# A two-layer diffusion trunk on one NeuronCore: the latent columns of layer 1 computed second, their steps run between the key and value units, and four modulation units placed in attention

## The chip, the cores and the metric

One core of one Trainium2 chip runs the whole program in one launch. The metric is device time in microseconds (us), the median of the runs, and every time below is from the kernel before unless it says otherwise. The engines are PE (TensorE: matmuls and transposes), DVE (VectorE), ACT (ScalarE), POOL (GpSimd) and SP (SyncE, which here only issues DMAs). Each engine works through its own instructions strictly in program order and meets the others at semaphores.

## The reference, cut to what matters

Two layers over 256 image tokens and 256 context tokens of 1024 features. Layer 0 is an even mixer and a dense feed-forward part, layer 1 an odd mixer and eight experts. The change lies in the odd mixer and in the modulation vectors of layer 1:

```python
# odd mixer: h, hc are the modulated tokens of image and context
p, pc = h @ w_in, hc @ w_in            # 1952 columns: q_c k_c v_c (512 each), cq 256, ckv 128, kr 32
q_d = rmsnorm(cq, gq) @ w_uq           # 4 heads of 64 + 32; the 32 are rotated
kv  = rmsnorm(ckv, gkv) @ w_ukv        # 4 heads: 64 of key, 128 of value
k_d = concat(key part, kr)             # kr is shared by the heads, rotated for image tokens
o_c = neighbourhood_attention(q_c, k_c, v_c, ..., rpb)   # 8 heads, with a position bias
o_d = attention(q_d, k_d, v_d)                           # 4 heads, without bias
y   = concat(o_c, o_d) @ w_out
# modulation: six vectors of 1024 per layer, for image and context
mod = silu(c) @ w_mod[l] + b_mod[l]
x   = x + g1 * rmsnorm(y);  h = rmsnorm(x) * (1 + sc2) + sh2;  x = x + g2 * rmsnorm(moe(h))
```

## The kernel before

**Weights as units.** Nearly all weights pass through SBUF in units of 1 MB (128 partitions x 2048 floats). `weight_units` (L100) lists them in order. SP loads them in that order into six raw slots: the load of unit r waits until unit r - 6 is released (L249 to L259). A unit of kind "split" is released when DVE has split it, a "mod" unit when PE has multiplied it, the "latent" unit when the last of its twelve products is done (semaphore `mla_full` at 12, L255). SP issues in order, so a load that waits holds back all that follow it, the bias loads among them.

**Split units.** A weight unit of 256 columns is split into a high and a low part so that three fast matmuls (L478 to L480) make one precise product. ACT writes the high half-unit (`act_split`, L451), DVE the low one (`dve_split`, L460). There are two split slots, so the splits of the unit after next wait for PE to finish this one (`half_free`, L442). PE runs a unit in `gemm_unit` (L493), ACT evicts its two PSUM banks and counts `od_evac`.

**The odd projection.** Eight units `od` 0 to 7: queries 0 and 1 (image tokens only, computed together while the modulated tokens arrive), keys 2 and 3, values 4 and 5, `cq` in 6 (image tokens only, so half the columns), `ckv` and `kr` in 7. A full unit streams 512 token columns, units 0, 1 and 6 stream 256. In the unit list the four modulation units 36 to 39 stand behind unit 1, 40 to 43 behind unit 7, then the latent unit (`w_uq` and `w_ukv`), then the output projection `odo`, then modulation units 44 to 47.

**Between projection and attention** each engine does, in order: ACT squares `cq` and `ckv` (L1039), PE sums them with a matmul by ones (L345), ACT takes the root (L340), DVE the reciprocal (L369) and scales. PE multiplies modulation units 40 to 43 (`pe_mod_rows`, L533; ACT copies the rows, L565; `pe_mod_turn`, L545, turns them), DVE adds the bias and forms the affine vectors. PE makes the twelve latent products (L1582 queries, L1586 keys, L1588 values), each waiting for ACT's eviction two back. Then eight rotations: PE matmul (L775), three DVE steps (L785 to L788): four queries, and the same rotated key once for each of four heads. Then attention starts.

**Attention** has 24 units in layer 1: 16 with the neighbourhood bias, 8 without. In iteration i PE runs the scores of unit i + 1 (L623), the transposes of unit i - 1 (L638) and, in odd iterations, the value product of a pair (L648). DVE scales and adds the bias (L698, L700), takes the maximum (L703, or L707 without bias), ACT the exponential (L663), DVE normalises (L726). The bias of each unit is fetched by two 64 KB DMAs on SP (`load_bias`, L851), which from the third unit on wait until the unit two back has used its buffer, and masked by POOL in two steps (L900, L902). `load_bias` stands ahead of modulation unit 44, that is behind all four `odo` units.

## Time and profile before

| | |
|---|---|
| median of 3 runs | 2098.78 us (2098.07 to 2099.05) |
| profiled execution, first to last instruction | 2095.1 us, 3.7 us below the median; its time outside that span is not shown |
| busy over the span | PE 1955.3 us (93%), DVE 1323.1 (63%), ACT 1112.9 (53%), POOL 28.5 (1%) |
| mean granted clock of PE | 0.964 |
| HBM read | 471.25 MB, 225 GB/s over the span |

The stages: layer 0 up to about 745 us, modulation and first norm of layer 1 to 755, odd projection to 831.5, small steps to 865.6, attention to 950.5, output projection, norms and router to about 1014, experts to the end. A share of busy time is a mean over stages with different limits; what a change in one stage is worth is read from what waits last there. "PEclk" is the clock that the throttle granted to PE: 1.00 is 2.4 GHz, 0.50 is 1.2 GHz. Matmuls are shown with their latency, so consecutive ones overlap a little, and a precise (float32) matmul shows as two records.

### The profile page before, as it was taken

To read this page: it belongs to the slowest core of one execution; us is meant where nothing else is said; L and a number is where in the kernel's file an instruction comes from. 1 tells how busy PE (TensorE), PEld (TensorE's weight loads), DVE (VectorE), ACT (ScalarE), POOL (GpSimd) and SP (SyncE) were. 2 spreads that over 40 slices of the span, in tenths; PEclk is the share of its full clock that TensorE was granted. 3 is DMA by queue.
4 is the path that set the end of the run, shared out by engine and by line. 5 is a ranking of instruction groups with operands and counts; after the bars stand their busy time and mean duration, and the time that the engine had idled before them with its cause. 6 is when DMAs were issued, how large, how long until landed. Compare 5 with 4: busy or idle time off the path is not lost.

```text
span 2095.1 us, 25387 instructions
## 1 busy us (share of the span) xinstructions
PE 1955.3 (93%) x9566; PEld 1537.2 (73%) x9566; DVE 1323.1 (63%) x1263; ACT 1112.9 (53%) x1126; POOL 28.5 (1%) x44
## 2 busy tenths in 40 slices
PE   5998798999999989888799999999999999999996
PEld 3876475888878768347788787887878878788785
DVE  2344735322323361464688888888888888888885
ACT  3533535222223252354477677767767777776773
POOL 0000000000000000120000000000000000000000
PEclk9998889999999999799699999999999999999998
DMA  9453153632222272221499898998989989899991
GB/s 316 139 161 121 32 189 101 201 99 84 100 86 96 72 233 72 78 63 62 159 355 364 317 355 314 360 361 319 362 306 371 363 304 368 307 360 344 331 368 43
DMA packets 263893, 473.27 MB, mean 226 GB/s; under 512 B 17112, under 2 KB 116368, under 8 KB 263824
## 3 DMA queue, kind: packets, MB, share of 16 engines
q1 hardware_dynamic: 262928, 469.31, 63.8%
q0 software_dynamic: 896, 3.02, 0.5%
q8 instruction: 46, 0.75, 0.2%
q14 instruction: 23, 0.19, 0.0%
HBM read 471.25 MB, written 1.05 MB: 225 GB/s over the span
## 4 chain that ended last, share of the span: by engine, by line
PE 82%; DVE 9%; ACT 4%; issue 4%; DMA 1%; DVEq 0%; SPq 0%; ACTq 0%
PE bank L478 23%; PE bank L480 23%; PE bank L479 23%; PE bank L345 2%; PE bank L541 2%; PE bank L648 2%; PE bank L1664 2%; DVE split_low L1414 2%; DMA raw_weights<-in_w_mod 1%; PE bank L1706 1%; PE bank L623 1%; DVE y L1401 1%; PE bank L638 1%; DVE overlay L419 1%; DVE small L707 1%
## 5 line engine op out<-in xcount | busy, mean ns | idle before, releaser
L1414 DVE TENSOR_TENSOR split_low<-raw_weights,split_high 128x2048 fp32r<-128x2048 f32 x224 | 511.6, 2287 | 59.5 <-ACT split_high L1113 58.6
L1113 ACT ACTIVATE split_high<-raw_weights 128x2048 fp32r<-128x2048 f32 x224 | 429.0, 1918 | 147.4 <-PE bank L480 147.3
L462 DVE TENSOR_TENSOR split_low<-raw_weights,split_high 128x1024 fp32r<-128x1024 f32 x118 | 143.9, 1225 | 330.4 <-ACT split_high L457 330.3
L478 PE MATMUL bank<-h_high,split_high 128*128 128x512 f32 (+1 forms) x848 | 326.2, 385 | 23.4 <-DVE h_low L392 10.6
L479 PE MATMUL bank<-h_low,split_high 128*128 128x512 f32 (+1 forms) x848 | 321.4, 379 | 0.0
L480 PE MATMUL bank<-h_high,split_low 128*128 128x512 f32 (+1 forms) x848 | 321.3, 379 | 0.0
L1414 DVE TENSOR_TENSOR h_low<-raw_weights,h_high 128x2048 fp32r<-128x2048 f32 x112 | 256.6, 2291 | 78.1 <-ACT h_high L1113 78.1
L478 PE MATMUL bank<-split_high,xe_high 128*128 128x512 f32 x672 | 271.7, 404 | 14.3 <-DVE split_low L1414 14.3
L480 PE MATMUL bank<-split_high,xe_low 128*128 128x512 f32 x672 | 266.2, 396 | 0.0
L479 PE MATMUL bank<-split_low,xe_high 128*128 128x512 f32 x672 | 266.1, 396 | 0.0
L1113 ACT ACTIVATE h_high<-raw_weights 128x2048 fp32r<-128x2048 f32 x112 | 214.7, 1917 | 43.0 <-PE bank L480 43.0
L457 ACT ACTIVATE split_high<-raw_weights 128x1024 fp32r<-128x1024 f32 x118 | 123.7, 1054 | 203.5 <-PE bank L480 199.5
L478 PEld LDWEIGHTS bank<-h_high,split_high 128*128 128x128 f32 x848 | 162.0, 191 | 57.7 <-issue 22.1
L479 PEld LDWEIGHTS bank<-h_low,split_high 128*128 128x128 f32 x848 | 162.1, 191 | 30.1 <-issue 1.2
L480 PEld LDWEIGHTS bank<-h_high,split_low 128*128 128x128 f32 x848 | 161.7, 191 | 29.4
L478 PEld LDWEIGHTS bank<-split_high,xe_high 128*128 128x128 f32 x672 | 127.0, 189 | 48.0 <-DVE split_low L1414 20.5
L480 PEld LDWEIGHTS bank<-split_high,xe_low 128*128 128x128 f32 x672 | 126.8, 189 | 30.3
L479 PEld LDWEIGHTS bank<-split_low,xe_high 128*128 128x128 f32 x672 | 127.1, 189 | 27.9
L478 PE MATMUL bank<-h_high,xe_high 128*128 128x512 f32 x224 | 89.2, 398 | 3.9 <-DVE h_low L1414 3.9
L478 PE MATMUL bank<-split_high,gt_high 128*128 128x512 f32 x224 | 89.2, 398 | 0.0
L480 PE MATMUL bank<-h_high,xe_low 128*128 128x512 f32 x224 | 88.6, 395 | 0.0
L480 PE MATMUL bank<-h_high,gt_low 128*128 128x512 f32 x224 | 88.5, 395 | 0.0
(236 smaller groups left out, 2711.7 us busy)
## 6 DMA issues: line engine op xcount, KB each, us to landing
raw_weights<-in_moe_w SPq DMA_DIRECT2D x336, 1024.0 KB, 7.1
raw_weights<-in_w_mod SPq DMA_DIRECT2D x48, 1024.0 KB, 6.8
raw_weights<-in_ffn_w SPq DMA_DIRECT2D x33, 1024.0 KB, 5.3
raw_weights<-in_ev_w_in SPq DMA_DIRECT2D x10, 1024.0 KB, 11.9
raw_weights<-in_od_w_in SPq DMA_DIRECT2D x8, 1024.0 KB, 9.7
raw_weights<-in_ev_w_out SPq DMA_DIRECT2D x4, 1024.0 KB, 11.2
raw_weights<-in_od_w_out SPq DMA_DIRECT2D x4, 1024.0 KB, 6.8
overlay<-in_rpb SPq DMA_DIRECT2D x32, 64.0 KB, 2.3
```

The costliest lines, as they stand in the source:

```text
L345: pe.matmul(n["sums"], ones, n["sq"][:, t % 2, :n["width"]], start=(t == 0), stop=(t == n["nt"] - 1)).then_inc(S("squares_used"), 1)
L419: dve.tensor_tensor(TMP[:, t % 2, :wd], n["src"](t), RS[:, :wd], ALU.mult)\
L457: act.activation(half_of(s, j, SPH[:, s % NSPLIT, :]), half_of(s, j, raw_of(r)), ACT.Copy)\
L462: dve.tensor_tensor(half_of(s, j, SPL[:, s % NSPLIT, :]), half_of(s, j, raw_of(split_at[s])), half_of(s, j, SPH[:, s % NSPLIT, :]).bitcast ...
L478: pe.matmul(ps, wh, xh, start=first, stop=False)
L479: pe.matmul(ps, wh, xl, start=False, stop=False)
L480: return pe.matmul(ps, wl, xh, start=False, stop=last)
L541: last = pe.matmul(PS[bank][32 * j:32 * j + 32, 256 * (i % 2):256 * (i % 2) + 256], SC[:, 4 * h + j, :], wt[:, 4 * h + j, :], start=(h == ...
L648: last = pe.matmul(pair_out(units, p)[0], u["v"][kt], PT[p % 2][:, kt, :], start=(kt == 0), stop=(kt == u["nk"] - 1))
L1113: act.activation(esplit(u)[0], RAW[:, u % NRAW, :], ACT.Copy).then_inc(S("e_high"), 1)
L1414: dve.tensor_tensor(lo, RAW[:, u % NRAW, :], hi.bitcast(F32), ALU.subtract)\
L1664: last = pe.matmul(PS[XBANK[r]][:, P * f:P * f + P], half[:, t, k:k + P], rhs, start=(n == 0), stop=(n == 3))
```

## The change

The units of the odd projection are computed in the order 0, 1, 6, 7, 2, 3, 4, 5. Everything that hangs on units 6 and 7 moves into the loop over the units, at positions p (0 to 7) of that order:

- ACT squares `cq` right after unit 6 (p = 2) and `ckv` after unit 7 (p = 3). PE sums `cq` ahead of the unit at p = 4 and `ckv` ahead of p = 5; root, reciprocal and scaling follow at the same positions.
- The rotary key is rotated once, on its own 32 rows (PE at p = 5, ahead of the unit; DVE behind it), and ACT copies the result to heads 1 to 3 at p = 6. Before, it was copied to four heads first and rotated four times.
- The latent products 0 to 7 run ahead of the unit at p = 6, products 8 to 11 and the four query rotations ahead of p = 7. Products now use PSUM banks 2 and 3.
- Attention on PE now waits for four rotations, the spread key, product 12's eviction and the last unit's eviction (`od_evac` 16).
- Modulation units 40 to 43 are multiplied inside attention, in iterations 4, 6, 10 and 12, ahead of the value product's place and behind the transposes; the first turn in iteration 10, the second in 16. ACT copies the rows in iterations 9 and 15, DVE adds bias and affine in iteration 21. The output projection waits for them.
- In the load order the latent unit stands behind the unit at p = 4, modulation units 40 to 43 behind the last unit; `load_bias` stands ahead of the third `odo` unit instead of ahead of modulation unit 44.

```diff
+OD_ORDER = (0, 1, 6, 7, 2, 3, 4, 5)
-    for s in range(8):
+    for s in OD_ORDER:
         units.append(("split", "od", cols(od, min(256 * s, OD_IN - 256))))
         if s == 1:
             units += mods(36, 40)
+        if s == 2:
+            units.append(("latent", "latent", [(0, (2, 384), w["mla_w_uq"][0].rearrange("(k p) n -> p k n", p=P)),
+                                               (768, (768,), w["mla_w_ukv"][0])]))
     units += mods(40, 44)
-    units.append(("latent", "latent", [(0, (2, 384), w["mla_w_uq"][0].rearrange("(k p) n -> p k n", p=P)),
-                                       (768, (768,), w["mla_w_ukv"][0])]))
...
# SP
-                if r == mod_at[44]:
+                if r == split_at[of["odo"][2]]:
                     load_bias()
...
+        KROT = KD[64:96, 0, CTX:TOK]
+        def pe_key_rope(pe):
+            pe.wait_ge(S("od_evac"), 8)
+            pe.matmul(PS[4][64:96, :SEQ], CON[64:96, C_R1 + 64:C_R1 + 96], KROT, start=True, stop=True)\
+              .then_inc(S("key_rot"), 1)
+        def dve_key_rope(dve):
+            t1, t2 = Y[64:96, 6, 0:256], Y[64:96, 6, 256:512]
+            dve.wait_ge(S("key_rot"), 1)
+            dve.tensor_tensor(t1, PS[4][64:96, :SEQ], TAB[64:96, 3, :], ALU.mult)
+            link(dve, dve.tensor_tensor(t2, KROT, TAB[64:96, 2, :], ALU.mult))
+            dve.tensor_tensor(KROT, t1, t2, ALU.add).then_inc(S("key_roped"), 1)
+        def act_key_spread(act):
+            act.wait_ge(S("key_roped"), 1)
+            for h in range(1, 4):
+                last = act.activation(KD[64:96, h, :], KD[64:96, 0, :], ACT.Copy)
+            last.then_inc(S("key_spread"), 1)
...
# ACT, loop over the units (act_latent evicts products i0 to i1 as before)
+            for g, p, s in run_od():
                 to(min(g + 1, of["od"][-1]))
+                if p == 4:
+                    act_root(act, N["cq"])
+                if p == 5:
+                    act_root(act, N["ckv"])
+                if p == 6:
+                    act_key_spread(act)
+                    act_latent(0, 8)
+                if p == 7:
+                    act_latent(8, 12)
...
+                if s == 6:
+                    act_squares(act, N["cq"])
+                if s == 7:
+                    act_squares(act, N["ckv"])
...
+                if i in (9, 15):
+                    act_mods(act, 20 + i // 15, 21 + i // 15, 3)
...
# DVE
+            for g, p, s in run_od():
+                to(min(g + 1, of["od"][-1]))
+                if p == 2:
+                    dve_mods(dve, 8, 10, 7)
+                    dve_affine(dve, 1, 1, 0.0, 16)
+                if p == 4:
+                    dve_latent("cq", V_GQ, 2)
+                if p == 5:
+                    dve_key_rope(dve)
+                    dve_latent("ckv", V_GKV, 1)
+                if p == 7:
+                    dve_rope(dve, 1, range(4))
...
+                if i == 21:
+                    dve_mods(dve, 10, 11, 1)
+                    dve_affine(dve, 1, 2, 1.0, 32)
...
# PE, loop over the units
+                if p == 4:
+                    pe.wait_ge(S("mod_evac"), 10)
+                    pe_sums(pe, N["cq"])
+                if p == 5:
+                    pe_sums(pe, N["ckv"])
+                    pe_key_rope(pe)
+                if p == 6:
+                    pe_latent(0, 8)
+                if p == 7:
+                    pe_latent(8, 12)
+                    pe.wait_ge(S("key_roped"), 1)
+                    pe_rope(pe, 1, lambda i: (S("mla_evac"), i + 1), range(4))
...
+            pe.wait_ge(S("roped1"), 4)
+            pe.wait_ge(S("key_spread"), 1)
+            pe.wait_ge(S("mla_evac"), 12)
+            pe.wait_ge(S("od_evac"), 16)
+            def mods_between(i):
+                if i in (4, 6, 10, 12):
+                    if i == 10:
+                        pe_mod_turn(pe, 20, 1)
+                    pe_mod_rows(pe, 40 + (4, 6, 10, 12).index(i), 3)
+                if i == 16:
+                    pe_mod_turn(pe, 21, 1)
```

## Rows read from the trace of the kernel before

**Rows 1.** The page, part 4: the chain that ended last, by engine.
```profile
PE 82%; DVE 9%; ACT 4%; issue 4%; DMA 1%; DVEq 0%; SPq 0%; ACTq 0%
```

**Rows 2.** Windows by stage: stretch, length, busy (instructions) of five engines, PEclk, DMA, GB/s.
```profile
769.62:831.52 61.90, 61.90 (x384) 55.76 (x384) 13.52 (x12) 16.09 (x23) 0.00 (x0) 1.00 0.30 98
831.52:865.65 34.13, 25.54 (x135) 12.02 (x134) 15.86 (x32) 11.91 (x23) 2.86 (x4) 0.91 0.32 101
865.65:950.51 84.86, 71.90 (x240) 35.51 (x240) 49.68 (x123) 37.71 (x84) 20.56 (x28) 0.84 0.18 47
1040.00:2095.00 1055.00, 1023.79 (x4678) 829.78 (x4676) 882.92 (x548) 738.19 (x507) 0.00 (x0) 0.99 0.90 328
```

**Rows 3.** Timeline, projection to attention: start, length, engine, line, [idle before <- releaser].
```profile
831.56 2.04 ACT L1036 ACTIVATE overlay<-bank 32x512 f32<-32x512 f32 x4 [4.87 <-PE bank L480]
834.19 2.50 PE L345 MATMUL bank<-y,constants 128*128 128x256 f32 x6 [2.66 <-ACT y L332]
...
838.49 3.34 DVE L369 RECIPROCAL y<-y 128x512 f32<-128x512 f32 x1
840.46 1.93 PE L541 MATMUL bank<-raw_weights,silu_c 128*32 128x256 f32 x32 [0.82 <-ACT mod_row_buffers L565]
842.32 1.95 PE L549 MATMUL bank<-constants,mod_row_buffers 128*128 128x2 f32 x16
844.13 3.67 PE L1582 MATMUL bank<-overlay,raw_weights 128*96 128x256 f32 x16
...
851.35 3.80 PE L1588 MATMUL bank<-raw_weights,overlay 128*128 128x512 f32 x8
855.83 1.10 PE L775 MATMUL bank<-overlay,constants 96*96 96x256 f32 x4 [0.69 <-ACT overlay L1053]
858.23 0.64 PE L775 MATMUL bank<-overlay,constants 96*96 96x256 f32 x2 [0.48 <-DVE y L785]
```

**Rows 4.** The unit loop: one wait (total, times, longest), and the opening splits.
```profile
PE bank L478 <- DVE split_low L462: 1.6, 1, 1.6
768.34 4.88 DVE L462 TENSOR_TENSOR split_low<-raw_weights,split_high 128x1024 fp32r<-128x1024 f32 x4 [2.08 <-ACT split_high L457]
```

**Rows 5.** Timeline: SP's issues, and POOL's first masking step.
```profile
838.61 3.34 SPq L816 DMA_DIRECT2D raw_weights<-in_od_w_out  x3
841.99 38.34 SPq L861 DMA_DIRECT2D overlay<-in_rpb  x12
851.89 0.72 POOL L900 TENSOR_TENSOR overlay<-overlay,constants 128x256 f32<-128x256 f32 x1 [808.62 <-DMA overlay<-in_rpb]
```

**Rows 6.** Attention's opening, and PE's gap before transposes at half and full clock.
```profile
865.65 3.78 PE L623 MATMUL bank<-overlay 64*128 64x512 f32 x4 [1.86 <-DVE overlay L788]
869.32 1.28 ACT L663 ACT_TABLE_LOAD   x1 [13.54 <-DVE small L703]
890.63 1.12 PE L638 MATMUL bank<-constants,y 128*128 128x128 f32 x4 [0.35 <-DVE y L726]
905.27 0.66 PE L638 MATMUL bank<-constants,y 128*128 128x128 f32 x4 [1.49 <-DVE y L726]
```

**Rows 7.** The chain in attention: start, length, what; transposes two units before those of rows 6.
```profile
880.51 1.12 PE bank L638 x4
...
898.50 0.66 PE bank L638 x4
```

**Rows 8.** Windows of the granted clock, attention of layer 0 and of layer 1.
```profile
194.00:210.00 16.00, 12.57 (x37) 5.83 (x37) 11.50 (x31) 8.02 (x24) 0.00 (x0) 0.50 0.00 1
864.00:893.00 29.00, 24.14 (x45) 9.62 (x46) 14.45 (x37) 9.31 (x19) 8.15 (x11) 0.50 0.14 28
894.00:950.00 56.00, 46.25 (x192) 25.16 (x191) 35.80 (x90) 27.90 (x65) 11.62 (x16) 1.00 0.21 57
```

**Rows 9.** Two gaps of PE (timeline) that half clock followed.
```profile
194.89 0.80 PE L623 MATMUL bank<-overlay 64*128 64x256 f32 x2 [2.32 <-DVE modulation L571]
954.79 0.42 PE L478 MATMUL bank<-h_high,split_high 128*128 128x256 f32 x1 [4.29 <-DVE split_low L462]
```

More of the change, by code:

```diff
@@ L615, in pair_out, with pe_attention @@
             return PS[OBANK[p % 2]][u["o"], :2 * P], (u["o"], t, slice(c, c + 2 * P))
-        def pe_attention(pe, a, units):
+        def pe_attention(pe, a, units, between=lambda i: None):
             def scores(i):
@@ L640, in pe_attention @@
                     last.then_inc(S(f"ptrans{a}"), 1)
+                between(i)
                 if i >= 3 and i % 2 == 1:
@@ L650, in pe_attention, with act_attention @@
                     last.then_inc(S(f"o{a}"), 1)
-        def act_attention(act, a, units):
+        def act_attention(act, a, units, between=lambda i: None):
             for i in range(len(units) + 3):
+                between(i)
                 if i < len(units):
@@ L680, in act_attention, with dve_attention @@
                     act.activation(HH[dst], src, ACT.Copy).then_inc(S("o_high"), 1)
-        def dve_attention(dve, a, units):
+        def dve_attention(dve, a, units, between=lambda i: None):
             lag = 3 + a
             for i in range(len(units) + lag):
+                between(i)
                 if i < len(units):
@@ L766, in ropes @@
             r, c, s = CON[0:96, C_R1:C_R1 + 96], TAB[0:96, 2, :], TAB[0:96, 3, :]
-            return [(QD[0:96, h, :], r, c, s) for h in range(4)] + [(KD[0:96, h, CTX:TOK], r, c, s) for h in range(4)]
+            return [(QD[0:96, h, :], r, c, s) for h in range(4)]
         def pe_rope(pe, l, ready, tiles=range(8)):
@@ L1015, in _, with act_latent @@
             act_modulate(act, N["n4"], 1, 0, 0)
-            for g, s in run("od"):
-                to(min(g + 1, of["od"][-1]))
+            def act_latent(i0, i1):
+                for i in range(i0, i1):
+                    act.wait_ge(S("mla_full"), i + 1)
+                    b = PS[2 + i % 2]
+                    if i < 4:
+                        act.activation(QD[0:96, i, :], b[0:96, :SEQ], ACT.Copy).then_inc(S("mla_evac"), 1)
+                    elif i < 8:
+                        act.activation(KD[0:64, i - 4, :], b[0:64, :], ACT.Copy).then_inc(S("mla_evac"), 1)
+                    else:
+                        act.activation(VD[:, i - 8, :], b[:, :], ACT.Copy).then_inc(S("mla_evac"), 1)
+            for g, p, s in run_od():
+                to(min(g + 1, of["od"][-1]))
+                if p == 4:
[7 more added lines that the diff above has]
+                    act_latent(8, 12)
                 for j in range(2):
@@ L1553, in _, with pe_latent @@
             pe_mods(pe, 36, 40, 5, 7)
-            for g, s in run("od"):
-                if s == 0:
+            r = latent_at
+            uq, ukv = raw_of(r)[:, 0:768].rearrange("p (k n) -> p k n", k=2), raw_of(r)[:, 768:1536]
+            def pe_latent(i0, i1):
+                for i in range(i0, i1):
+                    if i == 0:
+                        pe.wait_ge(S(f"raw{r % NRAW}"), need[r])
+                        pe.wait_ge(S("latent"), 1)
+                    if i == 4:
+                        pe.wait_ge(S("latent"), 2)
+                    if i >= 2:
+                        pe.wait_ge(S("mla_evac"), i - 1)
+                    else:
+                        pe.wait_ge(S("od_evac"), 4)
+                    b = PS[2 + i % 2]
+                    if i < 4:
+                        for k in range(2):
+                            last = pe.matmul(b[0:96, :SEQ], uq[:, k, 96 * i:96 * i + 96], CQ[:, k, :],
+                                             start=(k == 0), stop=(k == 1))
+                    elif i < 8:
+                        c = 192 * (i - 4)
+                        last = pe.matmul(b[0:64, :], ukv[:, c:c + 64], CKV, start=True, stop=True)
+                    else:
+                        last = pe.matmul(b[:, :], CKV[:, P * (i - 8):P * (i - 7)],
+                                         ukv.rearrange("p (h n) -> p h n", h=4)[:, :, 64:192], start=True, stop=True)
+                    last.then_inc(S("mla_full"), 1)
```

85 lines of the change are left out of this document (18 added, 67 removed).

## The prediction

> **What bounds the kernel now.** I read the page's chain first [rows 1]: TensorE (PE) carries 82% of the time that decides the end, and every share is an average over stages. So I cut the span around the change into stages [rows 2]. The reader is to see four things. While the units of layer 1's input projection run (769.62 to 831.52 us), PE is busy for 61.90 of 61.90 us, so work put in there is paid unless it replaces a wait. Between the last of these matmuls and the first score of attention lie 34.13 us with PE busy for 25.54: small dependent steps, all on the end's path. Attention takes 84.86 us, with PE busy 71.90 but at a mean granted clock of 0.84. The experts after it move 328 GB/s and hold PE at 97%; they follow attention in the program, so what is won before them should shift them as a block. Then I read the 34 us instruction by instruction [rows 3], the waits of the unit loop [rows 4], the DMA queue [rows 5], attention's opening and gaps [rows 6, 7] and the clock [rows 8, 9].
>
> **What the change takes away.** All of the 34.13 us between the last projection matmul and the first score: norm sums, four modulation units, twelve latent products, eight rotations. The loop of units itself keeps its matmuls; only their order changes. The one unit with 256 token columns (half as long as the others) now comes first after the opening pair. The loop is five full units and that half one, so 61.90 / 5.5 = 11.3 us for a full unit and 5.6 for the half. The splits of its successor must be ready after those 5.6 us. Now the four splits behind the opening pair run on VectorE from 768.34 to 773.2 and would be needed from about 775 on; only 1.6 us of waiting shows in the whole loop [rows 4]. I cost the reordering at 0, with up to 2 us if that cover fails.
>
> **What comes back inside the loop, on PE** (durations at full clock from [rows 3]):
> - Norm sums: the row says 2.50 us with a part at half clock and a short wait inside; I take 2.0. The squares are made two units earlier, under a matmul unit.
> - Key rotation: one matmul like those of the rotations, of which two take 1.10, so 0.55. Its three VectorE steps and the copies to the other heads lie beside the next unit.
> - Latent products 0 to 7: 7.2 us, from the first's start at 844.13 to the start of product 8 at 851.35. Before product 2, ScalarE must finish what it queues at the unit's end: an eviction (0.60), half a split (1.05), three copies of the rotated key (2.04 / 4 each, 1.53) and the first latent eviction (0.38), with handovers some 3.9 us. PE has two products, 1.75 us, to fill that; wait 2.1.
> - Latent products 8 to 11: 3.80.
> - Four query rotations: 855.83 to 858.23 + 0.64, so 3.0. They alternate with VectorE, and now stand ahead of the last unit.
> - Last eviction before the first score: 0.60 and handover, 0.8.
>
> Sum 2.0 + 0.55 + 7.2 + 2.1 + 3.8 + 3.0 + 0.8 = 19.5 us. The loop's end moves by that much, the 34.1 us go: **14.6 us won** before attention. The norm of the key latents is ready in time: reciprocal 3.34 plus scaling 0.75, behind a split (about 3.1) and the key rotation (1.3), makes 8.5 us after a unit's end, and PE asks for it some 12 us after. Cover 3.5 us; without it each late microsecond is paid.
>
> **What attention gets in exchange.**
> - Bias loads. They are issued on SP behind the weight units. Now three 1 MB units leave from 838.61 and the first bias DMAs at 841.99, and GpSimd can start masking at 851.89 [rows 5], 14 us before the first score. After the change, the third modulation unit waits for the raw slot of the latent weights, hence for latent product 11, and the bias loads wait on SP behind it, behind the fourth one and two output units. That is 4 MB instead of 3 once product 11 is done. From first issue to GpSimd it takes 13.3 us now; one more unit (1.05 MB) at the 328 GB/s of the experts' stage [rows 2] is 3.2, so 16.5. Product 11 ends 3.8 us into the stretch before the last unit; GpSimd starts at 20.3, and its two masking steps (0.72 each) make the bias ready at 21.8. VectorE asks for it after rotations, last unit, eviction and score: 3.8 + 3.0 + 11.3 + 0.8 + 1.0 = 19.9. **Cost 1.9 us**, bounds 0 and 5.
> - Modulation units. Two units are 32 records in 1.93 us (starting at 840.46), so 0.97 each, and two turns 1.95, so 0.97 each [rows 3]. They stand in even iterations, ahead of PE's gap before the next transposes. At full clock that gap is 1.49 us and swallows a unit; at half clock it is 0.35 and a unit takes 1.9 [rows 6]. So: iteration 4 (half clock) 1.6; iteration 6 between 0 and 1.6, I take 0.5; iteration 10, turn and unit, 0.4; iteration 12, 0; the turn in iteration 16, where the biasless heads leave gaps of about 0.3, 0.9; VectorE's bias add and affine in iteration 21, 0.3. ScalarE's two copies of 0.60 lie in its idle half. **Cost 3.7**, bounds 1.6 and 6.
> - Clock. From 864 to 893 the clock was granted at 0.50, that is 1.2 GHz, and from 894 on at 1.00, 2.4 GHz [rows 8]. It fell during the rotations, where PE worked in short pieces. A stretch of two units takes 10.12 us at half (880.51 to 890.63) and 6.77 at full clock (898.50 to 905.27) [rows 6, 7]. With the change, dense matmuls run up to the first scores, which start at full clock: the two took 3.78 us, so the one that VectorE waits for goes from 1.9 to about 0.9, 1.0 won. Then PE idles until the first exponential is done: VectorE's three steps (1.5), table load 1.28, exponential 0.9 [rows 6], less the second score that PE runs meanwhile (1.0), plus the late bias: 2.7 + 1.9 = 4.6 us. PE gaps of 2.32 us and of 4.29 us were each followed by half clock [rows 9]. So I expect the fall there. How long it lasts is the largest unknown: 16 us in the attention of layer 0 [rows 8], 28 us here. I take somewhat less than here, 1.5 us won; bounds 0 and 6.8.
>
> Attention: +1.9 + 3.7 - 1.0 - 1.5 = +3.1 us.
>
> Of the Trainium skill, "TensorE: Matmul & The Clock Gate", Part 1 ("What's actually happening"), says that the throttled clock is the default state and that activity releases it. Read plainly, attention with a busy PE would be released soon after its opening. The 29 us at 0.50 with PE busy for 24.14 of them [rows 8] say otherwise here, so the sum keeps the long stretch. By the page the result would be that of the first rival.
>
> **Sum.** -14.6 + 3.1 = -11.5 us. The profiled execution has a span of 2095.1 us, 3.7 below the median 2098.78; I take what lies around it as unchanged: 2098.8 - 11.5 = **2087.3 us**.
>
> **Rivals.**
> (a) The clock holds through attention's opening, or comes back quickly. For it: dense work right before, and 16 us in layer 0. Against it: every long gap seen brought a fall. At full clock from the start attention would be about 7.8 us shorter than now: the opening 1.95 (two scores at full clock), the stretches of two units up to 925 us 5.9 (10.12 - 6.77 for two of them, less for those that half clock touched in part). Modulations then cost 1.6. Time: 2098.8 - 14.6 + 1.9 + 1.6 - 7.8 = 2079.9. Chance 0.22.
> (b) More is given back: the latents are late for PE in the loop (beyond the 3.5 us cover), or the bias comes 5 us late and both early modulation units fall into half clock. Then 2.0 + 3.1 + 1.1 are added and the clock gains of 2.5 are gone: 2087.3 + 8.7 = 2096.0, within 0.2% of now. For it: SP and ScalarE are strictly in order, and several steps now hang on them. Chance 0.09.
> (c) Slower: half clock lasts through all 16 biased units, because PE's work there is now cut by more and longer gaps. Each microsecond at full clock becomes 10.12 / 6.77 = 1.5. From 894 to 925 that adds 16 us, and the modulations of iterations 10 to 16 leave their gaps, about 5.5. Time 2087.3 + 21.5 = 2108.8. It decides once half clock outlasts today's stretch by some 23 us (11.5 / 0.51). Against it: both attentions recovered by themselves. Chance 0.04.
> (d) The change does nothing: only if the loop had been waiting for weights and not PE; PE's 61.90 of 61.90 us speak against that. Chance 0.02, at 2098.8.
> The forecast itself: 0.63, with a range of its own of 2083 to 2092.
>
> **Chances and range.** About 0.2%, 4.2 us, can be told from no change here, so faster means below 2094.6. Faster: forecast, (a) and a small part of (b), 0.89; same: most of (b) and (d), 0.08; slower: 0.03. The range reaches to (a) and to the edge of (b): 2078 to 2094.5.
>
> **What would show it.** After the last projection matmul the first score should start within 1 us. In the loop PE should idle near 2 us once, behind the two first latent products, with ScalarE's eviction named. The latents stretch is right at 9.3 us. GpSimd's first masking step after the first score would prove the late bias; well before it would refute it. The clock row of attention's opening decides between the forecast and (a): half clock for 20 us or more, or under 10. A PE wait of over 0.5 us behind modulation units at full clock would break the claim that the gap swallows them. The prediction is wrong as a whole if the loop's matmuls themselves have gaps for splits or weights.

## The result and the profile after

| | before | after |
|---|---|---|
| median, on the same chip | 2098.91 us (2098.07 to 2102.95, 4 runs) | **2079.36 us** (2078.68 to 2082.3, 4 runs) |
| ratio | | **0.9911**, 95% interval 0.9894 to 0.9928 |
| profiled execution, first to last instruction | 2095.1 us | 2080.5 us (2082.3 as device time) |
| mean granted clock of it | 0.964 | 0.965 |

Inside the range of 2078.0 to 2094.5, but 7.9 us below the forecast, and almost exactly at the number of rival (a), 2079.9. Whether it came about as (a) says is a question for the trace. Two further sets of six runs of the unedited changed kernel, "again" and "again2" below, gave medians of 2082.86 and 2081.80. All 16 runs of the changed kernel have a mean of 2081.8, against 2097.2 for 45 runs of the kernel before in the later comparisons. So 15.3 us, good to about 1.8 us, is a better figure for the gain than the 19.5 of the first four against four.

The page of the kernel after, part 4, the chain that ended last by engine (as [rows 1]):

```profile
PE 82%; DVE 8%; ACT 4%; issue 3%; DMA 2%; SPq 0%; DVEq 0%; ACTq 0%
```

TensorE carries most of the chain as before. Windows of the kernel after (stretch, length, busy time and instructions of PE, PE's loads, DVE, ACT, POOL, then PEclk, DMA share, GB/s): from the first matmul of the third unit to the first score, attention, all that follows, and two pieces of attention:

```profile
753.27:850.66 97.39, 92.36 (x529) 75.48 (x529) 35.53 (x47) 39.86 (x68) 0.00 (x0) 0.98 0.34 109
850.66:935.92 85.26, 74.04 (x320) 38.09 (x320) 50.64 (x125) 38.68 (x86) 23.15 (x32) 0.88 0.26 72
935.92:2080.50 1144.58, 1096.25 (x5130) 896.62 (x5130) 928.26 (x648) 777.36 (x572) 0.00 (x0) 0.97 0.85 311
853.00:871.00 18.00, 13.56 (x27) 5.81 (x28) 9.72 (x23) 7.04 (x14) 6.93 (x11) 0.54 0.18 37
888.00:893.00 5.00, 4.71 (x14) 2.43 (x14) 2.91 (x7) 1.80 (x5) 1.45 (x2) 0.66 0.27 56
```

The same stretch up to the first score, and all behind attention, in the kernel before (its attention is in [rows 2]):

```profile
754.88:865.65 110.77, 100.58 (x614) 79.64 (x614) 38.96 (x58) 41.09 (x70) 2.86 (x4) 0.97 0.36 116
950.51:2095.10 1144.59, 1095.55 (x5130) 895.00 (x5130) 927.79 (x648) 777.49 (x572) 0.00 (x0) 0.97 0.86 311
```

Read these three by three. The loop with everything that now stands in it is 110.77 - 97.39 = 13.4 us shorter. Attention takes 85.26 against 84.86: only 0.4 us more, although it took in the modulation units. What follows is 1144.58 against 1144.59, so the gain before it does shift the rest as a block, as I had assumed. The spans of the two profiles differ by 14.6 us; the 1.6 us of it that are left come from a start at 753.27 instead of 754.88, ahead of anything the change touches; over all profiles below that start lies anywhere from 750.9 to 758.3.

The moved steps in the loop, timeline of the kernel after (start, length, engine, line, [idle before <- releaser]; compare [rows 3]):

```profile
796.72 1.02 PE L353 MATMUL bank<-y,constants 128*128 128x512 f32 x2
797.67 0.61 PE L805 MATMUL bank<-overlay,constants 32*32 32x256 f32 x2
...
809.23 1.89 PE L1628 MATMUL bank<-overlay,raw_weights 128*96 128x256 f32 x8
809.42 0.60 ACT L1077 ACTIVATE overlay<-bank 128x512 f32<-128x512 f32 x1 [3.90 <-PE bank L488]
809.92 1.05 ACT L465 ACTIVATE split_high<-raw_weights 128x1024 fp32r<-128x1024 f32 x1
810.99 1.66 ACT L818 ACTIVATE overlay<-overlay 32x512 f32<-32x512 f32 x3
812.67 0.65 ACT L1054 ACTIVATE overlay<-bank 96x256 f32<-96x256 f32 x2
813.11 3.38 PE L1628 MATMUL bank<-overlay,raw_weights 128*96 128x256 f32 x8 [1.99 <-ACT overlay L1054]
816.42 3.91 PE L1632 MATMUL bank<-overlay,raw_weights 128*64 128x512 f32 x8
...
831.86 3.69 PE L1634 MATMUL bank<-raw_weights,overlay 128*128 128x512 f32 x8
835.39 1.03 PE L786 MATMUL bank<-overlay,constants 96*96 96x256 f32 x4
```

The queue of SP, the bias and the opening of attention, same kernel and view (compare [rows 5] and [rows 6]):

```profile
835.58 0.99 SPq L847 DMA_DIRECT2D raw_weights<-in_w_mod  x2
836.62 4.24 SPq L847 DMA_DIRECT2D raw_weights<-in_od_w_out  x2
840.91 14.61 SPq L892 DMA_DIRECT2D overlay<-in_rpb  x7
...
850.66 1.95 PE L631 MATMUL bank<-overlay 64*128 64x512 f32 x4 [0.78 <-ACT overlay L1080]
851.03 0.72 POOL L931 TENSOR_TENSOR overlay<-overlay,constants 128x256 f32<-128x256 f32 x1 [808.51 <-DMA overlay<-in_rpb]
852.65 0.42 DVE L709 TENSOR_SCALAR y<-bank 128x256 f32<-128x256 f32 x1 [12.05 <-PE bank L631]
854.21 1.28 ACT L673 ACT_TABLE_LOAD   x1 [3.70 <-DVE small L714]
856.37 2.07 PE L631 MATMUL bank<-overlay 64*128 64x512 f32 x2 [3.76 <-ACT y L673]
...
872.55 1.07 PE L549 MATMUL bank<-raw_weights,silu_c 128*32 128x256 f32 x16
874.98 0.33 PE L646 MATMUL bank<-constants,y 128*128 128x128 f32 x1 [0.31 <-DVE y L737]
```

PE waits 1.99 us in the middle of the latent products, and the products behind it are slow: 3.38 us for what took 1.89 just before. It waits 0.78 before the first score and 3.76 after the second one. DVE's row names the score as the releaser, but four score records are done by 852.6 while the first, which DVE needs, is done near 851.7; what DVE really waited for is POOL's second masking step, which follows on the 0.72 us at 851.03. The bias was late by about 1.0 us. The third score takes 2.07 instead of about 1.1: the clock had fallen in the gap.

### The profile page after: what moved, and what is told of

It is laid out like the page before. It is cut to its first block, busy times and chain, and to the rows that moved or that the text cites. A ratio compares the mean times of both kernels' runs of the same rounds, so it can differ in the third digit from the quotient of the medians.

```text
span 2080.5 us, 25354 instructions
## 1 busy us (share of the span) xinstructions
PE 1948.2 (94%) x9560; PEld 1536.7 (74%) x9560; DVE 1321.1 (64%) x1254; ACT 1112.5 (53%) x1126; POOL 28.2 (1%) x44
## 4 chain that ended last, share of the span: by engine, by line
PE 82%; DVE 8%; ACT 4%; issue 3%; DMA 2%; SPq 0%; DVEq 0%; ACTq 0%
PE bank L486 23%; PE bank L488 23%; PE bank L487 23%; PE bank L353 2%; PE bank L657 2%; DMA raw_weights<-in_w_mod 2%; PE bank L1742 2%; DVE split_low L1470 2%; PE bank L549 1%; PE bank L631 1%; PE bank L1784 1%; PE bank L646 1%; DVE y L1457 1%; DVE overlay L427 1%; DVE residual L439 1%
## 5 line engine op out<-in xcount | busy, mean ns | idle before, releaser
L486 PE MATMUL bank<-h_high,gt_high 128*128 128x512 f32 x224 | 88.5, 395 | 0.0
## 6 DMA issues: line engine op xcount, KB each, us to landing
raw_weights<-in_ev_w_out SPq DMA_DIRECT2D x4, 1024.0 KB, 10.7
```

The source lines that it names most:

```text
L486: pe.matmul(ps, wh, xh, start=first, stop=False)
```

## The experiments

The questions: where the 13 to 15 us before attention come from; what the four modulation units cost inside attention and outside it; and whether half clock in attention, and not the work, explains the distance to the forecast. The first experiments undo, or do alone, one part of the change each. In the table "low" is the time at half clock worked out from a window: 2 x (1 - PEclk) x length. "Equal clock" takes the price of half clock away from attention: a stretch of two units takes 10.12 at half and 6.77 at full clock [rows 6, 7], so each low microsecond costs 3.35 / 10.12 = 0.33. PEclk has two digits, which makes that column good to 0.3 us; the price is that of the kernel before in its biased units, and is an estimate for every other stretch.

| kernel | median us (range; runs) | ratio to before, 95% | loop | attention (low) | attention at equal clock |
|---|---|---|---|---|---|
| before | 2097.2, 2097.1, 2095.8 in the three comparisons | | 110.8 | 84.9 (27) | 75.9 |
| changed | 2079.36 (2078.7 to 2082.3; 4) | 0.9894 to 0.9928 | 97.4 | 85.3 (20) | 78.5 |
| again | 2082.86 (2079.0 to 2089.7; 6) | 0.9903 to 0.9937 | 95.8 | 91.9 (37) | 79.7 |
| again2 | 2081.80 (2078.7 to 2084.6; 6) | 0.9916 to 0.9946 | 95.8 | 85.1 (20) | 78.3 |
| mods_front | 2086.11 (2083.8 to 2092.2; 6) | 0.9929 to 0.9964 | 104.1 | 81.6 (21) | 74.5 |
| mods_only | 2097.43 (2091.0 to 2102.0; 12) | 0.9982 to 1.0009 | 107.2 | 92.7 (43) | 78.6 |
| reorder_only | 2096.07 (2088.7 to 2102.5; 12) | 0.9971 to 1.0000 | 107.5 | 88.3 (39) | 75.4 |
| bias_early | 2079.83 (2075.7 to 2089.2; 6) | 0.9899 to 0.9952 | 96.9 | 82.0 (13) | 77.6 |
| spread_late | 2082.23 (2076.4 to 2085.6; 6) | 0.9896 to 0.9940 | 94.0 | 83.9 (17) | 78.3 |
| fill | 2084.14 (2082.2 to 2085.5; 6) | 0.9918 to 0.9957 | 97.4 | 88.8 (23) | 81.1 |
| rows_open4 | 2085.31 (2082.9 to 2088.2; 6) | 0.9921 to 0.9961 | 97.4 | 84.6 (14) | 80.1 |
| mods_empty | 2082.64 (2079.3 to 2089.0; 6) | 0.9918 to 0.9948 | 96.9 | 86.3 (28) | 77.2 |
| one_each | 2077.87 (2075.8 to 2081.0; 6) | 0.9899 to 0.9928 | 93.9 | 83.4 (20) | 76.8 |
| one_each_fill | **2073.33** (2073.2 to 2074.2; 5) | 0.9878 to 0.9907 | 94.0 | 79.1 (3) | 78.0 |

Loop and attention are those of the one profiled execution of each kernel, the median is over all its runs. The two must not be mixed: the profiled execution of "again", for one, is its slowest run.

### The changed kernel twice more

No edit. First comparison:

> The changed kernel once more, unedited, as the yardstick of this group. First theory (the small steps were replaced by dense work, all else is chance): about 19.5 us below the kernel before in the medians, and a profile whose parts before, in and after attention differ from the first one by no more than 2 us each, except where half clock falls elsewhere. Rival (the part of the gain that the two profiled executions do not show, some 5 us, is clock): this profile has less time at half clock in attention than the 21 us of the first, and a span 3 to 5 us shorter.

Third comparison:

> The changed kernel, unedited, as the yardstick of this group. First theory: 15 to 17 us below the kernel before in the medians, the spread of its runs (2079 to 2090 in the earlier group) going with the mean granted clock at 1.2 to 1.5 us for each 0.001. Rival (the spread is something else, DMA or the start): no such slope.

The latent products in the loop of "again" (timeline), and its attention (window):

```profile
811.64 1.89 PE L1628 MATMUL bank<-overlay,raw_weights 128*96 128x256 f32 x8
815.52 1.97 PE L1628 MATMUL bank<-overlay,raw_weights 128*96 128x256 f32 x8 [2.00 <-ACT overlay L1054]
817.42 3.69 PE L1632 MATMUL bank<-overlay,raw_weights 128*64 128x512 f32 x8
...
851.44:943.33 91.89, 81.65 (x320) 41.43 (x320) 49.12 (x125) 38.69 (x86) 23.21 (x32) 0.80 0.25 66
```

Attention of "again2":

```profile
852.72:937.80 85.08, 73.78 (x320) 38.17 (x320) 49.44 (x125) 38.70 (x86) 23.47 (x32) 0.88 0.26 72
```

In the loop the same wait of 2.00 us is there, and in "again2" too, but PE goes on at full clock (1.97 us for the next products). That is the 1.6 us by which their loops are shorter than the first one's. In attention, the same program with the same 320 matmuls takes 6.8 us more or less, with the clock at 0.80 and 0.88. That is a large part of the 10 us between the runs of one kernel. It is no accident of two profiles: over the runs of all kernels, each taken from its kernel's mean, the time falls by 1.3 us for each 0.001 of mean granted clock (1.35 over the 16 runs of the changed kernel, 1.25 over 45 of the one before; correlation -0.88, so the clock goes with about three quarters of the variance). The price fits: 0.001 of a span of some 2090 us is 4.2 us at half clock, and at 0.33 each these cost 1.4 us. From here on a kernel is judged by its runs, and a profile is used to price steps, at equal clock.

### The modulation units: in front of attention, and alone in it

mods_front is the changed kernel, with units 40 to 43 between the last rotation and the first score:

```diff
+            pe_mods(pe, 40, 44, 3, 1)
-            pe_attention(pe, 1, att1, mods_between)
+            pe_attention(pe, 1, att1)
...
+            act_mods(act, 20, 22, 3)
-            act_attention(act, 1, att1, mods_between)
+            act_attention(act, 1, att1)
```

> The changed kernel with modulation units 40 to 43 multiplied, copied and turned between the last rotation and the first score, instead of inside attention. If attention hides them, as forecast at full clock, this costs what stands on the path: four units 3.9, two copies with handovers 1.6, two turns 1.9 and VectorE's add, 7.6 us in all, less 1 to 3 that they cost inside attention: 5 to 7 us slower than the changed kernel. If they cost as much inside attention as outside, no difference. If they also keep the clock up at attention's opening (they fill its first gap's foreground), up to 3 us of that comes back.

Windows of mods_front, loop and attention:

```profile
752.33:856.45 104.12, 98.03 (x608) 79.57 (x608) 35.53 (x47) 42.17 (x71) 2.86 (x4) 0.98 0.32 103
856.45:938.01 81.56, 69.08 (x241) 34.69 (x240) 49.44 (x125) 36.56 (x84) 20.41 (x28) 0.87 0.28 75
```

and a step of its timeline:

```profile
855.32 1.28 ACT L673 ACT_TABLE_LOAD   x1
856.45 3.34 PE L631 MATMUL bank<-overlay 64*128 64x512 f32 x4
```

Standing in front, the units cost 7 to 8 us of loop (104.1 against 97.4 and 95.8), but the median only 3.2 more than "again" and 4.3 more than "again2" (the mean of its runs, 2086.8, is 5.0 above that of the 16). Attention pays part of it back, at equal clock 3.8 to 5.2 us: the bias is no longer late, the units no longer sit in it, and ScalarE loads its table for the exponential at 855.32, before the first score. In the kernels before and after, that 1.28 us load stands behind the wait for the first maximum [rows 6], on the path.

mods_only is the kernel before with the same four units moved into attention and nothing else (the bias loads also ahead of the `odo` units; the edit is that part of the diff of the change):

> The kernel before with one part alone: modulation units 40 to 43 moved into attention (same iterations), the bias loads ahead of the output units so that they don't wait for them; order, latents and rotations as before. The sum of the forecast gives the modulations 5.8 to 7.6 us of the 34 and a cost of 1.6 to 3.7 inside attention, so 2 to 6 us faster than before. If the part inside the loop is what counts and this one only moves work, within 2 us of before.

reorder_only is the kernel before with only the order of the units changed (all dependent steps stay behind the last unit):

```diff
+OD_ORDER = (0, 1, 6, 7, 2, 3, 4, 5)
-    for s in range(8):
+    for s in OD_ORDER:
```

> The kernel before with the order of the units alone: 0, 1, 6, 7, 2, 3, 4, 5, everything else behind the loop as before (sums now start without waiting for fresh squares). Forecast: the order costs nothing, and the squares of the latents have still to be made behind the loop, so within 1 us of before. If the short unit at position 2 starves PE of splits, 1 to 2 us slower.

Attention of mods_only, then a piece of reorder_only's attention and the whole:

```profile
863.04:955.75 92.71, 83.37 (x320) 41.90 (x320) 49.44 (x125) 38.68 (x86) 20.60 (x28) 0.77 0.31 88
```

```profile
859.00:901.00 42.00, 36.25 (x72) 14.84 (x72) 22.25 (x54) 13.09 (x27) 11.65 (x16) 0.51 0.12 26
862.34:950.59 88.25, 76.45 (x240) 37.23 (x240) 49.87 (x123) 37.69 (x84) 20.34 (x28) 0.78 0.17 45
```

mods_only wins 3.6 us of loop and nothing in the median: 12 runs, 1.0 within the interval. The expected 2 to 6 us did not come. Why the loop wins only 3.6, where mods_front pays 7 to 8 for the same units, is shown by the row of the first latent products (timeline of mods_only):

```profile
839.84 5.35 PE L1592 MATMUL bank<-overlay,raw_weights 128*96 128x256 f32 x16 [2.68 <-DVE overlay L1279]
```

In the kernel before, the modulation units lay over VectorE's reciprocal and scaling, and PE went from them to the latents without a wait [rows 3]. Taken away alone they leave 2.68 us of waiting for VectorE, and behind it the clock fell for a while: 5.35 us for products that take 3.67. In attention the units then cost 2.7 us at equal clock (78.6 against 75.9). The clock comes on top: the mean clock of the runs is 0.9602, the lowest of all kernels here (before 0.9622), which at 1.3 us for each 0.001 is 2.6 us, and the profile has 43 us of attention at half clock. Work and clock together paid the gain back. reorder_only gains 1.1 us, with an interval that touches 1: it costs nothing, as forecast, and brings next to nothing. So neither the new order nor the moved modulations carry the gain by themselves. What is left is the latent chain, now inside the loop: from reorder_only to mods_front it is 2096.07 - 2086.11 = 10 us (8.7 in the means). A part of that is work that is gone and not moved, since the key is rotated once and not four times: three rotations fewer, each 1.12 us of the chain before (0.64 and the gap of 0.48 [rows 3]). Moving the modulations into attention adds 3 to 5 on top, once the norms and latents stand under the units of the loop and nothing waits where the modulations stood.

### What the modulation units cost inside attention

mods_empty cuts PE's work for units 40 to 43 to one small matmul each and leaves waits, loads and copies (what it leaves uncomputed stands in the expectation):

> The changed kernel with PE's work for modulation units 40 to 43 inside attention cut to one tiny matmul for each unit and one for each turn; loads, ScalarE's copies and VectorE's steps stay. (This leaves a part of the modulation vectors of layer 1 uncomputed.) The forecast prices PE's part at 3.4 us, bounds 1.3 to 5.7: attention at equal clock 2 to 4 us shorter than in the changed kernel, about 75.5 us with no half clock against 79. If the gaps of PE swallow the modulations, under 1 us.

```profile
854.03:940.34 86.31, 72.68 (x252) 37.06 (x252) 49.87 (x125) 38.56 (x86) 23.27 (x32) 0.84 0.26 71
```

That window of its attention has 68 matmul records fewer than the changed kernel's, and PE is busy for 72.68 us instead of 74.04. The median, 2082.64, lies beside 2082.86 and 2081.80. At equal clock the profiles give 77.2 against 78.3 to 79.7, so 1.1 to 2.5 us; in the medians nothing. Either way it is below the 3.4 that I had put down for PE's part.

rows_open4 puts all four units into PE's opening gap, behind the first two scores:

```diff
             scores(0)
             scores(1)
+            between(0)
...
-                if i in (4, 6, 10, 12):
-                    if i == 10:
-                        pe_mod_turn(pe, 20, 1)
-                    pe_mod_rows(pe, 40 + (4, 6, 10, 12).index(i), 3)
+                if i == 0:
+                    for j in range(40, 44):
+                        pe_mod_rows(pe, j, 3)
+                if i in (4, 6):
+                    pe_mod_turn(pe, 18 + i // 2, 1)
```

> The changed kernel with the four modulation units 40 to 43 all in attention's opening gap (behind the second score), ScalarE's copies in iterations 0 and 1 and the turns in iterations 4 and 6. Two units (1.94 us), the copy and two more (1.94) make about 4.7 us against a gap of 3.76, so the third score starts 1 us late; against that nothing is left for the iterations 4 to 12. If the gap brings the fall of the clock, 3 to 6 us faster than the changed kernel; if not, within 1 us.

It is 2.4 to 3.5 us slower than the unedited kernel (2085.31). Its timeline shows a part of the reason:

```profile
857.49 0.60 ACT L573 ACTIVATE mod_row_buffers<-bank 128x512 f32<-128x512 f32 x1 [4.08 <-PE bank L549]
858.10 1.28 ACT L674 ACT_TABLE_LOAD   x1
```

In ScalarE's program the copy of the rows stands ahead of the first exponential. It waited for the second unit until 857.49, and the table load and the exponential, for which PE's third score waits, came after it. From first to third score it takes 6.71 us (853.56 to 860.27) instead of 5.71: 1.0 us, as expected for it. The other 1.4 to 2.5 us are not shown by any row; the units in the iterations 4 to 12, whose removal was to balance it, cost less there than I had put down. The gap on PE was free, the place in ScalarE's order was not.

### The two waits that the change added

bias_early puts the first two bias loads ahead of the third modulation unit on SP:

```diff
+                if r == mod_at[42]:
+                    load_bias(0, 2)
                 if r == split_at[of["odo"][2]]:
-                    load_bias()
+                    load_bias(2, NB_)
```

> The changed kernel with the bias loads of the first two attention units issued ahead of modulation unit 42, while the unit loop runs, instead of behind four 1 MB units. In the profile of the changed kernel VectorE takes the first bias 0.95 us after the first score was ready. If that wait is the load's, it goes: 0.9 us faster than the changed kernel, and PE's opening gap shrinks from 3.76 to about 2.8 us. If the shorter gap also spares the fall of the clock, 3 to 6 us faster. If the wait was something else, no change.

```profile
852.10 1.95 PE L631 MATMUL bank<-overlay 64*128 64x512 f32 x4 [0.78 <-ACT overlay L1082]
...
856.95 2.07 PE L631 MATMUL bank<-overlay 64*128 64x512 f32 x2 [2.89 <-ACT y L673]
```

From first to third score it takes 4.85 us instead of 5.71, and PE's gap is 2.89 instead of 3.76: the late bias cost 0.87 us. Its median is 2 to 3 us below the unedited one, which the spread of the runs does not tell apart.

spread_late puts ScalarE's three key copies behind the last latent eviction:

```diff
                 if p == 6:
-                    act_key_spread(act)
                     act_latent(0, 8)
                 if p == 7:
                     act_latent(8, 12)
+                    act_key_spread(act)
```

> The changed kernel with ScalarE's three copies of the rotated key behind latent product 11 instead of ahead of product 0. If these copies (1.66 us) are what PE waits for in its 1.99 us gap behind the first two products, the gap shrinks to about 0.3 us: 1.6 us faster than the changed kernel. If the eviction and the split ahead of them set the gap, under 0.5 us.

PE's wait of 1.99 us shrinks to 0.2 (the waits of PE over the loop: total, times, longest; the changed kernel first, then spread_late):

```profile
PE bank L1628 <- ACT overlay L1054: 2.0, 1, 2.0
PE bank L486 <- DVE split_low L470: 1.6, 1, 1.6
```

```profile
PE bank L1628 <- ACT overlay L1054: 0.2, 1, 0.2
```

The loop is 94.0 instead of 95.8 to 97.4, so the copies were the wait; the median does not resolve it.

### Holding the clock

fill adds 14 dense matmuls whose result nobody reads, right behind the first two scores:

```diff
             scores(1)
+            if a == 1:
+                for j in range(14):
+                    pe.matmul(PS[1][:, :], SPH[:, j % 2, 0:P], HH[:, j % KT, :], start=True, stop=True)
```

> The changed kernel with 14 dense matmuls (3.2 us, into an unused bank, results not used) in PE's opening gap of attention. They take time that PE otherwise idles. Theory that the gap brings the fall of the clock: attention then opens at 2.4 GHz and is 4 to 6 us shorter than with the 16 us at half clock now. Rival, the fall comes from how attention's own work loads PE: half clock as now, time within 1 us of the changed kernel or up to 0.5 us above.

```profile
850.20 3.47 PE L639 MATMUL bank<-h_high,split_high 128*128 128x512 f32 x14
853.78 1.12 PE L631 MATMUL bank<-overlay 64*128 64x512 f32 x2
```

The opening gap is filled and the next score runs at full clock, 1.12 us instead of 2.07. But the clock fell soon after, from 859 to 866, and again from 883 to 900. The median (2084.14) is 1.3 to 2.3 us above the unedited ones, and attention at equal clock is longer (81.1). Bridging one gap only postponed the fall, and the filler was paid. That the gap is not needed for the fall is seen in mods_front too: there PE runs from the last turn straight into the first scores, its longest gap behind the loop is 0.99 us, and the clock fell as the scores began (PE alone: window, length, busy time, PEclk, DMA, GB/s):

```profile
856.00:859.00 3.00, 3.00 (x9) 0.66 0.00 0
```

one_each has both small mends (bias_early, spread_late) and never more than one modulation step in an iteration:

```diff
                 if i in (4, 6, 10, 12):
-                    if i == 10:
-                        pe_mod_turn(pe, 20, 1)
                     pe_mod_rows(pe, 40 + (4, 6, 10, 12).index(i), 3)
-                if i == 16:
-                    pe_mod_turn(pe, 21, 1)
+                if i in (8, 14):
+                    pe_mod_turn(pe, 20 + i // 14, 1)
```

> The changed kernel with three edits: the first two bias loads early, the key copies late, and in attention one modulation item for each even iteration (units at 4, 6, 10, 12, turns at 8 and 14, ScalarE's copies at 7 and 13). The waits seen say 0.9 + 1.8 us for the first two; the turns no longer stand behind a unit or among the biasless heads, 1 to 1.5 us more. So 3.5 to 4.5 us faster than the changed kernel at equal clock. If the waits only move to the next in line, under 2.

The mean of its runs, 2077.9, is 3.9 us below that of the 16 unedited ones, its median 2077.87: as expected, and more than either mend alone shows. The loop is 93.9 instead of 95.8 to 97.4, attention at equal clock 76.8 instead of 78.3 to 79.7. How much of that belongs to the turns was not tried by itself.

one_each_fill adds filler matmuls to it in the first three iterations, behind the transposes (11, 5 and 5; their result is unused):

```diff
+                if i < 3:
+                    for j in range((11, 5, 5)[i]):
+                        pe.matmul(PS[1][:, :], SPH[:, 0, 0:P], SPH[:, 1, 0:512], start=True, stop=True)
```

> The kernel of one item for each even iteration, with dense filler matmuls in PE's gaps of iterations 0 (11), 1 and 2 (5 each). With the opening gap alone filled the clock held through it and fell some 5 us later, in iterations 1 to 3, where PE has no value products. Theory that PE's light load there is what brings the fall: now it holds beyond iteration 3, less than 10 us at half clock in attention, attention 3 to 5 us shorter than without filler. Rival (the fall comes anyway, with attention's own pace): 15 us or more at half clock as before, and the filler costs up to 1 us.

Attention of one_each; then of one_each_fill, whole and in three pieces:

```profile
847.40:930.81 83.41, 74.43 (x320) 38.15 (x320) 49.64 (x125) 38.81 (x86) 20.64 (x28) 0.88 0.26 73
```

```profile
848.06:927.11 79.05, 72.79 (x341) 39.38 (x341) 49.75 (x125) 38.80 (x86) 20.78 (x28) 0.98 0.28 77
848.06:880.00 31.94, 30.02 (x139) 15.11 (x139) 21.46 (x50) 15.06 (x32) 13.17 (x18) 1.00 0.18 39
880.00:883.00 3.00, 2.53 (x8) 1.61 (x9) 1.89 (x5) 1.14 (x3) 1.08 (x3) 0.55 0.21 44
883.00:927.00 44.00, 40.13 (x196) 22.66 (x194) 26.40 (x72) 22.59 (x52) 6.53 (x9) 0.99 0.36 108
```

21 matmuls more, and attention is 4.4 us shorter: 1.2 us longer at equal clock, but 17 us less at half. The median is 2073.33, 4.5 below one_each and 8.5 below the mean of all runs of the unedited changed kernel. Its five runs lie within 1.0 us of each other, where one_each spreads over 5.2 and "again" over 10.7. That is the strongest evidence for the clock as the main source of the spread: take the half clock out of attention's opening and the runs agree. It rests on five runs of one kernel.

## Why the prediction was right, and where it was off

**The 14.6 us before attention: right.** The stretch up to the first score is 13.4 us shorter in the first profile and 14.9 in the two others. Term by term, forecast against the kernel after: norm sum of `ckv` and key rotation together 1.5 (with 0.86 for `cq` 2.4 in all, against 2.55); latents 0 to 7, 11.0 against 9.3; latents 8 to 11, 3.5 against 3.8; rotations 2.6 against 3.0; last eviction 0.78 against 0.8. The wait behind the first two products is 1.99 us, forecast 2.1, and the row names the eviction that I had named. The one miss, the latents, is the clock: in "again", where it held, they took 9.5 us (811.64 to the end of the row at 817.42); in the first profile it fell behind the wait. The 110.77 that all three are set against is a single profile of the kernel before.

**The reordering at 0: right.** PE waits once for a split, 1.6 us (the second of the changed kernel's two waits above), as in [rows 4], and reorder_only costs nothing.

**Late bias: mechanism right, size off.** POOL's first masking step starts at 851.03, 0.4 us after the first score, which is the order I had named as proof. The term was 1.9; it measured 0.95 in the kernel after and 0.87 by bias_early. From the end of product 11 to POOL's first step I had 16.5 us; it took 15.5 (835.58 to 851.03).

**Modulation units: too dear.** I charged 3.7 us. mods_empty gives 1.1 to 2.5 at equal clock and nothing in the medians. The unit in iteration 4, which I charged with 1.6 as at half clock, ran at full clock in the kernel after (1.07 us at 872.55), and PE's gap behind it was still 0.31: swallowed. The two iterations with the next unit in them take 6.57 us (874.98 to 881.55), the two after them, which hold none, 6.74 (to 888.29). No wait of over 0.5 us stood behind a unit at full clock.

**The clock: the fall came, the reason given for it did not hold.** My two clock terms, 2.5 us, stand for some 7.6 us less at half clock than the 27 of before, so for about 20. The whole of attention has 20, 37 and 20 us in the three profiles of the unedited kernel. The test that I had set was on its opening alone, 20 us or more against under 10, and there the half clock lasted 16, 20 and 16 us: between the two, nearer to the forecast. So rival (a)'s number came out in the first four runs and its mechanism did not: the clock did not hold. That is chance. What I got wrong is the picture of one fall, brought by one long gap, with one length. With the gap filled it fell all the same some 5 us later (fill), and in mods_front it fell with no gap to bring it. It also falls again later (888 to 892 in the kernel after, 889 to 906 in "again"), at places that differ from run to run, and the attention of a single profile is a draw from a wide range, the [rows 8] of before included. Over many runs, the changed kernel's mean clock is 0.9654 against 0.9622; at 1.3 us for each 0.001 that is worth 4.2 us over the whole kernel. Some 0.9 of it lie in the loop (0.98 against 0.97 there, so 2.7 us less at half clock), which leaves attention about 3.3 where I had 2.5.

**Sum.** 15.3 us gained over all runs, less 14.4 before attention (the mean of the three profiles), leaves attention at about -1 where I had +3.1. The difference of 4 is made of 1.0 for the bias, 1.2 to 2.6 for the modulations and about 0.8 for the clock, 3.0 to 4.4 in all. That split is worked out, not measured piece by piece: the medians of bias_early and mods_empty resolve neither of the first two alone. The rest of the 7.9 us, some 4, is the scatter of four runs against four.

**Base.** I said that the profiled execution lay 3.7 us below the median for what lies around its span. Only 1.8 us lie around it (2082.3 less 2080.5, and 1.7 to 2.0 in every run here); the other 1.9 must be that this execution was a quick one. It did not matter, since the difference was subtracted from the median.

**The page's rule.** The Trainium skill, "TensorE: Matmul & The Clock Gate", Part 1 ("What's actually happening"), lets activity release the throttle. The runs of this case agree only in part: reorder_only stood at half clock for some 40 us with PE busy in 36.25 of 42.00, so being busy with attention's work did not release it here; while filler matmuls in three iterations kept the clock at 1.00 for 32 us.

What stays open: what brings a fall, and why the falls come at different places in each run, or not at all. Filler was tried in these places and amounts only, and behind three iterations only on top of one_each. And the table load of 1.28 us, which mods_front takes off the path before the first score, was not tried on top of one_each_fill.

## What to carry to other kernels

Steps that run one behind the other between two dense stages cost their full latency; spread over the units of the stage before, each costs only its own time on the bound engine and the waits that are left, here 20 us instead of 34. Ask of work in such a chain what it covers: moved away alone it uncovers the wait that it filled (2.68 us in mods_only), and half clock took another part of that gain. A gap on the bound engine is only free for work whose helpers also have a free place in their order. Where the runs of a kernel spread by 5 to 10 us, plot time against granted clock before believing a single profile. A few dense matmuls that compute nothing may be worth more than the next reordering: 21 over three iterations were worth 4.5 us, 14 behind the first two scores cost 1.3 to 2.3.

## What was not expected of the hardware

- The same wait in the middle of a dense loop, 1.99 and 2.00 us, was followed by half clock in one profile of the unedited kernel and not in the two others. Windows of the kernel after and then, for the same place, of "again":

```profile
810.00:820.00 10.00, 8.01 (x22) 3.31 (x20) 1.22 (x1) 5.71 (x12) 0.00 (x0) 0.83 0.00 0
```

```profile
815.00:820.00 5.00, 4.48 (x14) 1.88 (x14) 0.00 (x0) 2.66 (x7) 0.00 (x0) 1.00 0.00 0
```

  I had taken long gaps for a sure fall and put down nothing for this one of 2 us; it fell in one profile of three, and that is part of why one program has many times.

- The same program on the same data differs by 10.7 us over the six runs of "again" and by 14.8 over 45 runs of the kernel before. Some three quarters of the variance go with the granted clock, at 1.3 us for each 0.001. Five runs with the opening of attention filled differ by 1.0.
- Half clock in attention began with a gap of 3.76 us on PE (the kernel after), some 5 us behind a filled one (fill), and in mods_front with no gap over 1.0 us.
- More work on the bound engine made the kernel 4.5 us faster (one_each to one_each_fill: 21 matmuls more, 17 us less at half clock).
